# Four up tiles instead of two along the x1 chain, row scales from a matrix of ones, and tiles that leave PSUM unscaled

## The reference

```python
def rms_norm(x, g):
    xf = x.astype(jnp.float32)
    y = xf * lax.rsqrt(jnp.mean(xf * xf, axis=-1, keepdims=True) + NORM_EPS)
    return (y * g.astype(jnp.float32)).astype(x.dtype)
...
def block_tail(x, mix, g_mix_post, g_ffn_pre, g_ffn_post, w_up, w_down):
    x = x + rms_norm(mix, g_mix_post)
    h = rms_norm(x, g_ffn_pre)
    f = jnp.square(jax.nn.relu(h @ w_up)) @ w_down
    return x + rms_norm(f, g_ffn_post)
```

## Time and profile before

| what | value |
| --- | --- |
| median of 3 runs (lowest to highest) | 893.11 us (892.37 to 893.71) |
| the profiled execution's own time | 894.82 us |
| its span, first to last instruction | 893.0 us |
| PE busy | 865.8 us, 97% of the span |
| DVE busy | 474.3 us, 53% |
| ACT busy | 303.6 us, 34% |
| POOL busy | 69.0 us, 8% |
| mean granted TensorE clock, share of full | 0.988 |

### The profile page before, as it was taken

The page is one execution under the profiler, slowest core; times in us unless marked ns, Lnnn a source line. Parts: engine busy times, 40 slices in busy tenths (PEclk is TensorE's granted clock), DMA queues, the critical chain, the costliest instruction groups (busy, mean ns, idle before and its releaser), DMA issues.

```text
span 893.0 us, 16412 instructions
## 1 busy us (share of the span) xinstructions
PE 865.8 (97%) x6866; PEld 850.1 (95%) x6866; DVE 474.3 (53%) x729; ACT 303.6 (34%) x448; POOL 69.0 (8%) x53
## 2 busy tenths in 40 slices
PE   6999999999999999999996899999999999999997
PEld 6999999999989999999995899999999999999997
DVE  6325779776735546656426654774433443334434
ACT  5211645354531112335323342123311332123432
POOL 1000101100020000000224400000000000000122
PEclk9999999999999999999996999999999999999999
DMA  9322212221313131123231022232222222322212
GB/s 311 105 95 94 86 59 72 88 90 59 96 48 101 54 101 49 54 95 95 95 94 49 18 79 95 95 94 95 82 64 89 94 94 94 94 91 66 80 48 101
DMA packets 77405, 77.28 MB, mean 87 GB/s; under 512 B 2912, under 2 KB 75120, under 8 KB 77360
## 3 DMA queue, kind: packets, MB, share of 16 engines
q1 hardware_dynamic: 68416, 70.53, 24.5%
q10 hardware_dynamic: 8304, 3.95, 1.6%
q0 software_dynamic: 640, 2.17, 0.7%
HBM read 71.64 MB, written 4.99 MB: 86 GB/s over the span
## 4 chain that ended last, share of the span: by engine, by line
PE 92%; DVE 5%; issue 1%; DMA 1%; ACT 1%; SPq 0%; DVEq 0%; ACTq 0%
PE acc L715 76%; PE wk L715 3%; PE wk L739 3%; PE wk L844 3%; DVE act_lo L1372 1%; DMA x_nat<-in_x_prompt 1%; PE wk L805 1%; PE wk L806 1%; PE wk L914 1%; DVE scaled L1353 1%; PE wk L922 1%; DVE w_lo L1065 1%; PE wk L912 0%; PE acc L1043 0%; PE acc L1045 0%
## 5 line engine op out<-in xcount | busy, mean ns | idle before, releaser
L452 ACT ACTIVATE w_hi<-w_raw 128x1024 fp32r<-128x1024 f32 x123 | 130.4, 1060 | 473.8 <-PE acc L715 455.5
L715 PE MATMUL acc<-act_hi,w_hi 128*128 128x272 f32 x1200 | 254.6, 294 | 10.8 <-DVE act_lo L1372 8.6
L715 PE MATMUL acc<-act_hi,w_lo 128*128 128x272 f32 x1200 | 249.8, 290 | 0.0
L715 PE MATMUL acc<-act_lo,w_hi 128*128 128x272 f32 x1200 | 249.1, 289 | 0.0
L715 PEld LDWEIGHTS acc<-act_hi,w_hi 128*128 128x128 f32 x1200 | 190.2, 190 | 16.0 <-DVE act_lo L1372 10.0
L715 PEld LDWEIGHTS acc<-act_lo,w_hi 128*128 128x128 f32 x1200 | 190.3, 190 | 0.0
L715 PEld LDWEIGHTS acc<-act_hi,w_lo 128*128 128x128 f32 x1200 | 188.9, 190 | 0.0
L1065 DVE TENSOR_TENSOR w_lo<-w_raw,w_hi 128x1024 fp32r<-128x1024 f32 x123 | 151.7, 1233 | 35.5 <-ACT w_hi L452 35.0
L715 PE MATMUL acc<-mid_hi,w_hi 128*128 128x272 f32 x480 | 99.0, 287 | 0.0
L715 PE MATMUL acc<-mid_hi,w_lo 128*128 128x272 f32 x480 | 98.7, 288 | 0.0
L715 PE MATMUL acc<-mid_lo,w_hi 128*128 128x272 f32 x480 | 98.6, 287 | 0.0
(11 more groups left out here) (219 smaller groups left out, 985.4 us busy)
## 6 DMA issues: line engine op xcount, KB each, us to landing
w_raw<-in_w_in SPq DMA_DIRECT2D x44, 512.0 KB, 4.4
w_raw<-in_w_ff_up SPq DMA_DIRECT2D x32, 512.0 KB, 4.7
w_raw<-in_w_ff_down SPq DMA_DIRECT2D x32, 512.0 KB, 4.0
w_raw<-in_w_o SPq DMA_DIRECT2D x8, 512.0 KB, 4.5
x_nat<-in_x_prompt SPq DMA_DIRECT2D x4, 512.0 KB, 5.7
...
```

Source lines behind the costliest of these rows:

```text
L452: act.activation(w_hi[:, v % 2], w_raw[:, v // 2, :, P * (v % 2):P * (v % 2) + P], ACT.Copy).then_inc(hi_ready, 1)
L715: ins = pe.matmul(dst[:, n, 0:HALF], w[:, k, :], h[:, HALF * n:HALF * n + HALF], start=begin, stop=end)
```

## The change

PE computes up tiles 0 to 3 together along the x1 chain: for each row tile the products of `act_hi` with all four high and low weights start at `h2_hi`, those of `act_lo` at `h2_lo`. They go to four places in PSUM (`wk_halves[0]`, `acc[0]`, `acc[1]`, `wk_halves[1]`). All four weight splits (`first_hi`, `first_lo`) are made while the last tiles of `w_o` run. ACT copies the four sums out of PSUM unscaled into `early`, and DVE applies relu and scale from there.

For both norms PE multiplies a 128 x 128 matrix of ones with `sqsum` and the last square (`sum_over`), which leaves the sum over all features on every partition; ACT takes the root of 544 columns, and DVE the reciprocal of 544 columns (`rstd_over`). The epsilon comes from the value that `sqsum` is filled with. The sums of the second norm stand in the middle of up tile 4. The additions to `xT` are all on DVE.

```diff
+        first_at = [z_at + 4 * T * s for s in (Z_RK, Z_RV, Z_RG)]
+        first_hi = [place(f"first_hi{q}", [P, KT, P], fr, at=first_at[q])[:] for q in range(3)] + [w_hi_third[:]]
+        first_lo = [place(f"first_lo{q}", [P, KT, P], fr, at=first_at[q] + 8 * T)[:] for q in range(3)] + [w_lo_third[:]]
...
+        early = [part_a[:], part_b[:], merged[:, 0, :], merged[:, 1, :]]
+        std = relu2[:, 0, :]
...
-            order.after(pool.memset(sqsum[:], 0.0))
-            for m in range(KT):
-                if m % 2:
-                    pool.wait_ge(scaled_ready, m // 2 + 1)
-                    pool.tensor_tensor(xT[:, m, :], xT[:, m, :], scaled[:, m % 4, :], ALU.add).then_inc(x1_odd, 1)
-                if m > 1:
-                    add_square(2, m - 2)
-            add_square(2, KT - 2)
+            order.after(pool.memset(sqsum[:], EPS * D / P))
+            for m in range(KT - 1):
+                add_square(2, m)
...
+            def first_split(q):
+
+                act.wait_ge(w_in_sem[q // 2], 32 * (G_FFN + 1))
+                act.activation(first_hi[q], w_raw[:, q // 2, :, P * (q % 2):P * (q % 2) + P], ACT.Copy).then_inc(hi_ready, 1)
+
             for m in range(KT):
-                act.wait_ge((x1_even, x1_odd)[m % 2], m // 2 + 1)
+                g, j = G_WO + m // 4, m % 4
+                if m < KT - 2:
+                    split_ahead(g, j)
+                if m == KT - 3:
+                    first_split(0)
+                    first_split(1)
+                if m < KT - 1:
+                    evacuated(act, g, j)
+                    y = y_mix[:, m, :]
+                else:
+
+                    act.wait_ge(mm_done, 4 * g + j + 1)
+                    y = acc[1][:, :, 0:HALF]
+                act.wait_ge(sq_added, m + 1)
+                to = sq[:, m % 2, :]
+                act.activation(to if m < KT - 1 else halves(to), y, ACT.Square).then_inc(sq_ready, 1)
+                if m == KT - 2:
+                    first_split(2)
+                    first_split(3)
+
+            def std_over(norm):
+
+                act.wait_ge(sum_mm, norm)
+                act.activation(halves(std), wk_halves[0][:, :, 0:HALF], ACT.Sqrt, scale=1.0 / D).then_inc(std_ready, 1)
+
+            std_over(1)
...
+                act.wait_ge(x1_ready, m + 1)
                 act.activation(act_hi[:, m, :], xT[:, m, :], ACT.Copy, scale=gains[:, 2, m:m + 1]).then_inc(h2_hi, 1)
...
-            root(2)
+                if m == KT - 4:
+                    split_hi(4 * G_FFN + 4, 0, 32 * (G_FFN + 2))
+            dst = [wk_halves[0], acc[0], acc[1], wk_halves[1]]
+            for q in range(4):
+                act.wait_ge(mm_done, 4 * G_FFN + q + 1)
+                act.activation(halves(early[q]), dst[q][:, :, 0:HALF], ACT.Copy).then_inc(early_read, 1)
+            split_hi(4 * G_FFN + 5, 1)
+            std_over(2)
...
-                    if not (first and j < 2):
+                    if not first:
...
+            def sum_over(norm):
+
+                for src, count, value in ((sqsum[:], sq_added, squares_added(norm, KT - 1)), (sq[:, 1, :], sq_ready, KT * norm)):
+                    pe.wait_ge(count, value)
+                    for n in range(2):
+                        ins = pe.matmul(wk_halves[0][:, n, 0:HALF], ones[:], src[:, HALF * n:HALF * n + HALF],
+                                        start=count is sq_added, stop=count is sq_ready)
+                ins.then_inc(sum_mm, 1)
...
-            feature_sum(1, squares_added(1, KT - 1), KT)
-            spread(1)
-
-
-
-            for k in range(KT):
+            sum_over(1)
+
+            pe.wait_ge(lo_ready, 4 * G_FFN + 4)
+            pe.wait_ge(acc_free, 4 * G_FFN + 2)
+            pe.wait_ge(std_ready, 2)
+            dst = [wk_halves[0], acc[0], acc[1], wk_halves[1]]
+
+            def first_product(q, k, w, h, start=False, stop=False):
+
+                for n in range(2):
+                    ins = pe.matmul(dst[q][:, n, 0:HALF], w[:, k, :], h[:, HALF * n:HALF * n + HALF], start=start, stop=stop)
+                return ins
+
+            for k in range(KT - 1):
+                pe.wait_ge(h2_hi, k + 1)
+                for q in range(4):
+                    first_product(q, k, first_hi[q], H_HI[k], start=k == 0)
+                    first_product(q, k, first_lo[q], H_HI[k])
                 pe.wait_ge(h2_lo, k + 1)
-                for j in range(2):
-                    if k == 0:
-                        pe.wait_ge(lo_ready, 4 * G_FFN + j + 1)
-                        pe.wait_ge(acc_free, 4 * G_FFN + j + 1)
-                    ins = products(acc[j], w_hi[:, j], w_lo[:, j], k, H_HI[k], H_LO[k], k == 0, k == KT - 1)
-                    if k == KT - 1:
-                        ins.then_inc(mm_done, 1)
-            feature_sum(2, squares_added(2, KT - 1), 2 * KT)
-            pe.wait_ge(lo_ready, 4 * G_FFN + 3)
-            for k in range(KT):
-                if k == 3:
-                    spread(2)
-                ins = products(wk_halves[1], w_hi_third, w_lo_third, k, H_HI[k], H_LO[k], k == 0, k == KT - 1)
-            ins.then_inc(mm_done, 1)
-
-            pe.wait_ge(acc_free, 4 * G_FFN + 4)
-            column_tile(G_FFN, 3, H_HI, H_LO)
+                for q in range(4):
+                    first_product(q, k, first_hi[q], H_LO[k])
+            pe.wait_ge(h2_lo, KT)
+            for q in range(4):
+                first_product(q, KT - 1, first_hi[q], H_HI[KT - 1])
+                first_product(q, KT - 1, first_lo[q], H_HI[KT - 1])
+                first_product(q, KT - 1, first_hi[q], H_LO[KT - 1], stop=True).then_inc(mm_done, 1)
+
+            def second_norm(k):
+
+                if k == KT // 2:
+                    pe.wait_ge(early_read, 1)
+                    sum_over(2)
+
+            for j in range(4):
+                if j < 2:
+                    pe.wait_ge(early_read, 2 + j)
+                column_tile(G_FFN + 1, j, H_HI, H_LO, before=second_norm if j == 0 else None)
...
+            def rstd_over(n):
+
+                dve.wait_ge(std_ready, n + 1)
+                order.after(dve.reciprocal(rstd[:], std))
...
+            def first_low(q):
+
+                dve.wait_ge(hi_ready, 4 * G_FFN + q + 1)
+                dve.tensor_tensor(first_lo[q], w_raw[:, q // 2, :, P * (q % 2):P * (q % 2) + P], first_hi[q].bitcast(fp), ALU.subtract)\
+                    .then_inc(lo_ready, 1)
+
+            for m in range(KT):
+                g, j = G_WO + m // 4, m % 4
+                dve.wait_ge(mm_done, 4 * g + j + 1)
+                if m == KT - 1:
+                    dve.wait_ge(sq_ready, KT)
+                copy(halves(y_mix[:, m, :]), acc[j % 2][:, :, 0:HALF]).then_inc(acc_free, 1)
+                if m < KT - 2:
+                    split_ahead(g, j)
+                for q in {KT - 3: (0, 1), KT - 2: (2, 3)}.get(m, ()):
+                    first_low(q)
+            rstd_over(1)
+
+            def scale(m):
+
+                order.after(dve.scalar_tensor_tensor(scaled[:, m % 2, :], y_mix[:, m, :], gains[:, 1, m:m + 1], rstd[:], ALU.mult, ALU.mult))
+
+            def add(m):
+
+                dve.tensor_tensor(xT[:, m, :], xT[:, m, :], scaled[:, m % 2, :], ALU.add).then_inc(x1_ready, 1)
 
...
-            pair(0)
-            h2_low(0)
-            for p in range(1, KT // 2):
-                pair(p, between=(lambda: h2_low(2 * p - 2)) if p > 1 else None)
-                h2_low(2 * p - 1)
-            h2_low(KT - 2)
+            for m in range(KT):
+                scale(m)
+                if m:
+                    h2_low(m - 1)
+                add(m)
             h2_low(KT - 1)
-            norm(2, between=lambda: split_ahead(G_FFN, 1), keep=True)
+            split_lo(4 * G_FFN + 4, 0)
+            split_lo(4 * G_FFN + 5, 1)
+            rstd_over(2)
...
+                    if first:
+                        dve.wait_ge(early_read, j + 1)
+                        src = halves(early[j])
+                    else:
+                        dve.wait_ge(mm_done, 4 * g + j + 1)
+                        src = acc[j % 2][:, :, 0:HALF]
+                    dve.scalar_tensor_tensor(halves(relu[:, j % 2, :]), src, 0.0, halves(rstd[:]), ALU.max, ALU.mult).then_inc(acc_free, 1)
 
...
-                if first:
-
-                    evacuate(0)
-                    evacuate(1)
-                    hidden_low(0)
-                    hidden_low(1)
-                for j in range(2 if first else 0, 4):
+                for j in range(4):
                     evacuate(j)
-                    split_ahead(g, j)
+                    if not first:
+                        split_ahead(g, j)
```

More of the change, by code:

```diff
@@ L294, in build @@
         ORDER = (3, 2, 0, 1, 4)
-        SUM_COL = 1000
         def x_psum(t):
@@ L764, in feature_sum, with spread @@
                 ins.then_inc(sum_mm, 1)
-            def spread(norm):
-                pe.wait_ge(tok_rstd_ready, norm + 1)
+            def sum_over(norm):
[5 more added lines that the diff above has]
```

(49 more changed lines are left out.)

30 lines of the change are left out of this document (7 added, 23 removed).

## The result

| kernel | median us (lowest to highest) | ratio to before, 95% interval |
| --- | --- | --- |
| before, 20 runs beside it | 893.65 (892.04 to 896.16) | 1 |
| changed, 20 runs | 895.15 (894.0 to 898.07) | 1.0017 (1.0009 to 1.0025) |

A forecast was written before the change was run, and what follows sets the result against it. PE bounds the kernel, so time moves only where PE stands still or runs slowly. The x1 part -11.7, second norm's sums +1.9, wait +8.5 and low clock +1.8 give +0.5 us: median 893.6 us, range 887.3 to 896.8.

The forecast's parts named there:

- slow: Rival for both norms: the DVE reciprocal takes 8.3 ns a column, 4.7 us, so +2.5, 895.6 us; chance 0.27.
- The x1 part: Up tiles 0 to 3 along the x1 chain: they end earlier than before, winning 11.7 us.
- The wait: Ahead of up tile 6: PE waits 8.5 us for its weight split, late in DVE's list.
- low clock: Behind PE's wait ahead of up tile 6: the clock is low again and costs 1.7 to 1.8 us.
- The reciprocal: In each norm, 544 columns on DVE: 3.7 us at 6.5 ns a column, each microsecond counting twice.
- quick: Rival for both norms: the reciprocal runs a column a cycle, 0.73 us, so -5.4, 887.7 us; chance 0.18.
- The row tile: In the x1 chain: DVE's scale, act_lo and add with one POOL block of 1.25 take 3.34 us.
- The rival with less blocking: x1 chain: POOL adds while DVE waits, a row tile takes 2.6 us; -1.0, 892.1 us; 0.10 with another rival.
- immunity: In the x1 chain: scaled, now reading rstd in SBUF, can be blocked by POOL; included in the 3.34 us.
- the prediction's last sign: Ahead of up tile 6: without PE's wait for w_lo of about 8 us, the kernel is about 10 us faster.
- norm 1: From the end of w_o's products to the first scale: sums, root and reciprocal, scale starting at 480.0, not 480.4.
- from there to the split: From the four tiles' end at 509.6 through second norm and early tiles to up tile 6's split at 532.0.

The follow-up runs named there:

- e3: Changed kernel with a DVE copy of 544 columns in place of both long reciprocals, so the norms scale by the root: 889.10 us.
- e1: Changed kernel with weight splits for up tiles 6 and 7 ahead of most early tiles, early tiles paired, tiles 6 and 7 summed in free PSUM: 884.89 us.
- e4: Changed kernel without POOL's seven additions of squares in the x1 chain, their counter still raised: 893.33 us.
- e5: Changed kernel with both weight splits early and early tiles in pairs, but up tiles 6 and 7 still summed in acc[0] and acc[1]: 892.62 us.

## Why the prediction was right, point by point

- **The time alone doesn't decide.** +1.5 us lies halfway between the forecast's +0.5 and the +2.5 of the rival slow, and 895.15 is nearer to slow's 895.6. It is the trace that tells them apart, term by term.
- **The two opposite terms.** Both were there. The x1 part ended 36.98 us after `w_o` (508.80 - 471.82), before 47.6 (521.3 - 473.7): it won 10.6, forecast 11.7. The wait was 8.3, forecast 8.5. e1 took the wait away and got back 10.8 us by the distances, against the 10.3 that wait and low clock were given.
- **The reciprocal.** 3.55 us, forecast 3.7. The rate is (3.55 - 0.165) / 542 = 6.2 ns a column. That settles the rivals quick (0.73) and slow (4.7). That I came so near was luck. The trace of before had more small reciprocals than I used, and they don't lie on a line:

```profile
L1301 DVE RECIPROCAL gn_rstd<-gn_std 128x4 f32<-128x4 f32 x4 | 0.7, 180 | 1.4 <-ACT gn_std L609 1.4
...
L1120 DVE RECIPROCAL tok_rstd<-tok_rstd 128x3 f32<-128x3 f32 x1 | 0.2, 179 | 0.3 <-ACT tok_rstd L482 0.3
```

  Four columns take 163 or 180 ns, and on one line it goes from 165 to 179 ns with the third column, 14 ns, and to 190 with two more, 5.5 ns each. So the small ones give no rate, 4.7 us was no upper end, and 6.5 ns was a choice, with about 6 us of the time hanging on it (e3). The Trainium skill has the divide run with a repeat count of 8 ("VectorE: DVE Perf Modes", First, the fixed hardware budget) and as a chain through all eight slices ("Vector Engine (DVE) Microarchitecture Reference", 3.2 Anatomy of a single slice). The estimates made from these, 4.7 us if the first means eight cycles a column and 0.7 if the second means one column a cycle, both miss the measured 3.55.
- **The row tile**, 3.46 to 3.48 us against 3.34: seven times 0.13 is 0.9, most of the miss of 1.1. The last 24 products took 3.3 us and not 3.0 (505.49 to 508.80), about the rest. The rival with less blocking had 2.6 for a row tile and is out too. The block was even a little shorter than the 1.25 I took from the row of 1.93: the addition's 1.87 is 1.15 over its own 0.72. What I had too small was the scale with its wait for `act_hi`, 0.97 from start to start (482.92 to 483.89) and not 0.80.
- **Which instruction is blocked** was wrong. The prediction said `scaled` would lose its immunity. It takes 0.78 in every row tile; POOL's addition always begins after it, and the block falls on the addition to `xT`. So no row here shows what `scaled` does beside POOL. The sum didn't depend on it.
- **Which engine decides the x1 part.** DVE does, by 2.0 us (e4), forecast 1.5.
- **The low clock behind the wait**, 2.1 us against 1.8. PE stopped at 522.7 and the clock fell at about 525.
- **The second wait under the first** was not in the prediction: without the split, PE would have waited for `acc[0]` (e5). It was hidden, so it changed no number. But the prediction's last sign, a kernel about 10 us faster if there is no wait for `w_lo`, holds only with this second wait gone as well. Against the changed kernel and by the last column, e5 without the wait for `w_lo` is 2.6 us faster, and e1 with neither wait 9.9.

In the sum: norm 1 -0.1, the x1 chain and its tail +1.2, from there to the split -0.3, the low clock +0.3, and rounding, which makes about +1.1 on the forecast +0.5. The medians' +1.5 agrees.
